# A hybrid decoder step: the selective keys of the sample tokens gathered by an on-chip list, and the differential pages loaded by SyncE

## The reference

```python
# selective (DSA): 8 heads, 2 key heads of 64; indexer with 4 heads of 64
ki_all = concat([gather_pages(cache_ik, page_table), ki])
idx, valid = select_keys(indexer_scores(qi, wi, ki_all), qpos, n_keys, 256)   # top 256 of each token
k_sel = gather_selected(cache_k, page_table, ka, idx, past)
v_sel = gather_selected(cache_v, page_table, va, idx, past)
return dsa_core(qa, k_sel, v_sel, valid, qpos[None, :, None] - idx, bias_a)

# differential: 4 heads of 2 x 64, all keys
k_all = concat([gather_pages(cache_k, page_table), kb])
v_all = concat([gather_pages(cache_v, page_table), vb])
logits = einsum('bqhcd,bkhcd->bhcqk', q, k) * 64 ** -0.5 + bias(distance)
p = softmax(where(causal, logits, -inf))
w = p[:, :, 0] - lam * p[:, :, 1]
o = rmsnorm(einsum('bhqk,bkhe->bqhe', w, v), subln_g) * (1 - lam_init)
```

## Time and profile before

| | us |
|---|---|
| median of three runs | 2603.62 |
| lowest and highest run | 2590.98, 2606.52 |
| span of the profiled execution | 2590.7 |
| PE busy | 2312.3 |
| DVE, ACT, POOL busy | 1103.6, 766.2, 660.5 |
| selective-and-sample stage, in the span | 565 to 1335 |

### The profile page before, as it was taken

How to read it: one execution, slowest core, us unless ns; L and a number is a source line. 1 busy time by engine, 2 the same in 40 slices (tenths; PEclk the granted TensorE clock), 3 DMA queues, 4 the chain that set the end, 5 groups by cost and what they waited for, 6 DMA issues and landing times. The chain is left out here.

```text
span 2590.7 us, 32530 instructions
## 1 busy us (share of the span) xinstructions
PE 2312.3 (89%) x12169; PEld 1549.6 (60%) x12189; DVE 1103.6 (43%) x2687; ACT 766.2 (30%) x2065; POOL 660.5 (25%) x703
## 2 busy tenths in 40 slices
PE   7999997767777878788789898899999999999999
PEld 5644443443455455555444445548888888888887
DVE  5489998742445533333322212352443343371001
ACT  3551345653444444444421013311111111110000
POOL 1451223123544445433301010013222121201110
PEclk9999998988889889998889999999999999999999
DMA  4211101025888778765540014111111111122221
GB/s 140 73 60 70 38 9 65 1 82 188 275 277 269 234 266 281 257 213 193 173 162 28 33 49 163 34 67 34 50 34 50 34 50 40 44 65 74 74 63 39
DMA packets 147603, 281.75 MB, mean 109 GB/s; under 512 B 13479, under 2 KB 82775, under 8 KB 147447
## 3 DMA queue, kind: packets, MB, share of 16 engines
q0 software_dynamic: 48384, 176.18, 20.2%
q1 hardware_dynamic: 80774, 90.50, 10.6%
q10 hardware_dynamic: 18288, 12.98, 1.7%
HBM read 261.68 MB, written 17.94 MB: 108 GB/s over the span
## 5 line engine op out<-in xcount | busy, mean ns | idle before, releaser
L634 PE MATMUL PS<-region 128*128 128x512 f32 (+5 forms) x864 | 327.7, 534 | 1.8 <-DMA region<-w_in 1.8
L2784 PE MATMUL PS<-region,ffn_w 128*128 128x264 f32 x1408 | 323.1, 388 | 1.6 <-PEq L2234 1.6
L2784 PEld LDWEIGHTS PS<-region,ffn_w 128*128 128x128 f32 x1408 | 269.2, 191 | 48.4 <-issue 1.9
L2004 ACT COPY region<-PS 128x512 f32<-128x512 f32 x352 | 197.2, 591 | 212.6 <-PE PS L1868 72.2
L634 PEld LDWEIGHTS PS<-region 128*128 128x128 f32 (+1 forms) x864 | 152.7, 181 | 161.2 <-issue 140.9
L2784 PE MATMUL PS<-region,side 128*128 128x264 f32 x1056 | 245.0, 389 | 1.8 <-POOL side L2741 1.8
L1875 PE MATMUL PS<-ident_f,region 128*128 128x128 f32 x1024 | 170.7, 316 | 82.4 <-ACT region L2004 44.1
L2784 PEld LDWEIGHTS PS<-region,side 128*128 128x128 f32 x1056 | 200.0, 191 | 35.8 <-POOL side L2741 1.9
L1875 PEld LDWEIGHTS PS<-ident_f,region 128*128 128x128 f32 x1024 | 133.5, 162 | 117.0 <-issue 76.3
L931 DVE TENSOR_SCALAR_CACHE_REDUCE mask<-score,cand 128x384 bf16<-128x384 f32 (+2 forms) x198 | 180.9, 942 | 3.4
L1109 POOL DMA_INDIRECT region<-cache_b_k,gather_b x128 | 120.4, 941 | 212.0 <-PE PS L1875 177.8
(11 more groups left out here) (448 smaller groups left out, 4017.7 us busy)
## 6 DMA issues: line engine op xcount, KB each, us to landing
ffn_w<-w_gate SPq DMA_DIRECT2D x11, 1024.0 KB, 5.4
ffn_w<-w_up SPq DMA_DIRECT2D x11, 1024.0 KB, 5.5
region<-w_in SPq DMA_DIRECT2D x4, 2048.0 KB, 7.9
ffn_w<-w_down ACTq DMA_DIRECT2D x7, 704.0 KB, 5.6
region<-x_prompt ACTq DMA_DIRECT2D x8, 512.0 KB, 7.1
region<-x_prompt SPq DMA_DIRECT2D x8, 512.0 KB, 10.6
mem_keys<-cache_mem_k SPq DMA_DIRECT2D x8, 512.0 KB, 5.0
mem_values<-cache_mem_v SPq DMA_DIRECT2D x8, 512.0 KB, 8.0
```

Source lines behind the costliest of these rows:

```text
L634: last = nc.tensor.matmul(M.PS[0:n, s % 3, 0:chunks[j].width], XT[:, c, t * P:t * P + n], w[j % 2][:, c, 0:chunks[j].width], start=(c == 0 ...
L2004: nc.scalar.copy(dst, M.PS[0:dst.shape[0], T0 + x % 2, 0:dst.shape[1]]).then_inc(t_read, 1)
L2784: last = nc.tensor.matmul(M.PS[:, bank, 0:TW], left[:, c, :], right[:, c, :], start=begin and c == 0, stop=(c == KH - 1), skip_group_check ...
```

## The change

Of the selective cache only three things are still read: the last page of each sequence ("near", 128 keys, with the new tokens in one chunk), and for each sample token the rows of its kept keys among the other 31 pages, 256 slots a token. A list of their row numbers is made on the chip: DVE writes the pool row number plus one of every kept key (0 elsewhere), takes out the eight largest of each of 128 partitions 32 times, counts how many each segment has, shifts the four segments' lists by the counts of the segments ahead in eight halving steps, and PE sums and turns them into columns of `ids`. These steps are "z" (41 of them); "c" and "z" steps now stand three to a chunk. POOL gathers with `ids` 128 rows of 512 B at a time: four "sets", one for each of four selective chunks (two tokens x 256 slots of four sequences), 32 gathers a set, and 16 for the near pages. The 18 selective chunks become six. Slots without a key, and the other tokens' slots, are masked by the matmul as before.

The differential pages are loaded by SP. For each page its number is loaded into a register, and a DMA brings the whole page to 128 partitions, one key of 2 KB a partition; two pages make the 256 keys of a sequence in a chunk, so a chunk takes 16 DMAs of 256 KB and 8 register loads. Keys stand now in order of pages and no longer in pairs, so the bias of the last chunk is added to the second page's columns by one matmul. The waits are those of the gathers before; the buffers stay.

The diff, cut to what the text speaks of:

```diff
-RKB, RKA, RKI = 2, 8, 16
-NCB, NCA, NCI = PAST // (P * RKB), PAST // (P * RKA), PAST // (P * RKI)
+RKB, RKI = 2, 16
+NCB, NCI = PAST // (P * RKB), PAST // (P * RKI)
...
+PAGES = PAST // PAGE
+FARW = SEGW - PAGE
@@ Setup
+        sp.dma_start(M.pages[:], io["page_table"][:]).then_inc(M.pages_loaded, 16)
...
-        if 2 <= s < 5:
-            n, rk, table = (("b", RKB, M.gather_b), ("a", RKA, M.gather_a), ("i", RKI, M.gather_i))[s - 2]
+        if s == 2:
+            link(nc.vector.tensor_scalar(M.page_rows[:], self.pt_f.rearrange("p (b i) -> p b i", i=PAGES)[:, :, PAGES - 1],
+                                         float(PAGE), K("page_row"), ALU.mult, ALU.add))
+            link(nc.vector.tensor_copy(M.gather_n[:], M.page_rows[:]))
...
+        if s == 4:
+            n, rk, table = "i", RKI, M.gather_i
@@ selective_and_sample_stage
-                       lambda step: 0.5 if step[0] in "kspof" and step[1] in selective else 1.0, lambda step: 1.0)
+                       lambda step: {"c": 0.5, "z": 0.0}.get(step[0], 2.0 if step[0] in "kspof" and step[1] in selective
+                                                             else 1.0), lambda step: 1.0)
@@ Walk
+    ROUNDS = TOPK // 8
+    LISTED = ROUNDS + 8
...
-        for kind, n_chunks in (("B", NCB), ("A", HALVES * NCA)):
+        for kind, n_chunks in (("B", NCB), ("A", 2)):
...
-        cut = iter(range(33))
+        cut = iter([("c", r) for r in range(33)] + [("z", r) for r in range(self.LISTED + 1)])
         for n in range(end + 1):
             keys = [("k", n + 1, j) for j in range(1 if self.new(n + 1) else 4)] if n < end else []
-            self.steps += keys[:3] + [("p", n)] + keys[3:] + [("o", n)] + [("c", r) for r in itertools.islice(cut, 1)]
+            self.steps += keys[:3] + [("p", n)] + list(itertools.islice(cut, 1)) + keys[3:] + [("o", n)]
+            self.steps += list(itertools.islice(cut, 1))
             if n < end:
-                self.steps += [("s", n + 1)] + [("c", r) for r in itertools.islice(cut, 1)]
+                self.steps += [("s", n + 1)] + list(itertools.islice(cut, 1))
@@ sample_attention: gpsimd
+        def near(b):
+            gather(near_k[:, b, :], near_loaded, rows_a[0], M.gather_n, b)
+            gather(near_v[:, b, :], near_loaded, rows_a[1], M.gather_n, b)
+
+        def chosen(x, v, j):
+
+            out, arrived = (set_values_at(x, j), set_values[x]) if v else (set_keys_at(x, j), set_keys[x])
+            for q in range(4):
+                t, half = 2 * (x % 2) + q // 2, q % 2
+                gather(out[:, q * P:(q + 1) * P], arrived, rows_a[v], ids,
+                       half * NS + DEC_T * (4 * (x // 2) + j) + t)
...
-        keys(0)
-        values(0)
...
+        eng.wait_ge(listed, 2)
+        for b in range(DEC_B):
+            near(b)
+        for v in range(2):
+            for j in range(4):
+                chosen(0, v, j)
+        eng.wait_ge(pv_done, walk.units[last - 2] + 1)
+        for v in range(2):
+            for j in range(4):
+                chosen(1, v, j)
+        for j in range(4):
+            eng.wait_ge(t_full, fill["k", walk.units[last], j, 1] + 1)
+            chosen(2, 0, j)
+        for j in range(4):
+            chosen(2, 1, j)
+        eng.wait_ge(pv_done, walk.units[last] + 1)
+        for v in range(2):
+            for j in range(4):
+                chosen(3, v, j)
@@ sample_attention: sync
+        def unit(u):
+
+            kind, g, c = chunks[walk.units[u]]
+            last = u == walk.n_units - 1
+            ids_b = {}
+            for v in range(2):
+                for j in range(4):
...
+                    elif v == 0:
+                        eng.wait_ge(t_full, fill["k", walk.units[u - 1], j, 1] + 1)
...
+                    elif j == 0:
+                        eng.wait_ge(pv_done, walk.units[u - 1 if last else u - 2] + 1)
+                    out, arrived = (values_at if v else keys_at)(u, j)
+                    for i in range(2):
+                        if v == 0:
+                            b = 4 * g + j
+                            ids_b[j, i] = eng.value_load(M.pages[b:b + 1, 2 * c + i:2 * c + i + 1], min_val=0,
+                                                         max_val=n_pool - 1)
+                        eng.dma_start(out[:, i * 512:(i + 1) * 512],
+                                      pages_b[v][bass.ds(ids_b[j, i], 1)].rearrange("o s f -> (o s) f")
+                                      ).then_inc(arrived, 16)
...
-                eng.wait_ge(mask_ready, 1)
+                eng.wait_ge(t_full, fill["k", walk.sets[0], 3, 0] + 1)
             else:
-                eng.wait_ge(pv_done, walk.units[-1] + 1)
+                eng.wait_ge(pv_done, walk.sets[1] + 1)
@@ sample_attention: tensor, the selective far chunks
+                for j in range(4):
+                    nc.tensor.matmul(M.PS[32 * j:32 * j + 32, L0, :], M.QBA[:, 4 * g + j, :], kt[:, j, 0:CH],
+                                     start=True, stop=True)
+                eng.wait_ge(listed, 2)
+                last = nc.tensor.matmul(out, M.tok_to_row_b[0:32, g, :], mask[0:32, c * CH:(c + 1) * CH], start=False,
+                                        stop=True, skip_group_check=True)
@@ sample_attention: vector
+        def list_kept(step):
+
+            r = step[1]
+            if r == 0:
...
+                link(nc.vector.tensor_tensor(work[:, 0:SEGW], work[:, 0:SEGW], score[:, 0:SEGW], ALU.mult))
+            elif r <= walk.ROUNDS:
+                eight = lists[0][:, 8 * (r - 1):8 * r]
+                link(nc.vector.max(eight, work[:, 0:SEGW]))
+                link(nc.vector.match_replace(work[:, 0:SEGW], eight, work[:, 0:SEGW], 0.0))
+            elif r == walk.ROUNDS + 1:
+                nc.vector.tensor_scalar(lists[1], lists[0], 0.0, 0.0, ALU.is_gt, ALU.add, accum_out=count[:, 0:1]
+                                        ).then_inc(counted_kept, 1)
...
+            if walk.ROUNDS + 3 <= r <= walk.ROUNDS + 6:
+                for k in (2 * (r - walk.ROUNDS - 3), 2 * (r - walk.ROUNDS - 3) + 1):
+                    a, b, far = lists[k % 2], lists[(k + 1) % 2], 1 << k
+                    link(nc.vector.tensor_scalar(b, a, stay[:, k:k + 1], None, ALU.mult))
+                    last = nc.vector.scalar_tensor_tensor(b[:, far:TOPK], a[:, 0:TOPK - far], bits[:, k:k + 1],
+                                                          b[:, far:TOPK], ALU.mult, ALU.add)
...
+            elif r == walk.LISTED:
...
+                nc.vector.tensor_copy(ids[:], slots_f).then_inc(listed, 1)
```

More of the change, by code:

```diff
@@ L1604, in new, with near @@
         return self.chunks[n][2] < 0
+    def near(self, n):
+        return self.new(n) and self.chunks[n][0] == "A"
     def first(self, n):
@@ L1858, in turn_keys @@
             kind, g, c = chunks[n]
+            if walk.near(n):
+                eng.wait_ge(near_loaded, 16 * 2 * DEC_B)
+                t = bank(("k", n, j, 0))
+                for q in range(4):
+                    last = nc.tensor.transpose(t[:, q * P:(q + 1) * P], near_k[:, 4 * g + q, :], K("ident"))
+                last.then_inc(t_full, 1)
+                return
             if walk.new(n):
                 return
[L1861 to L1863 removed]
             if kind == "A":
+                x = walk.sets.index(n)
+                keys = set_keys_at(x, j)
+                eng.wait_ge(set_keys[x], 16 * 16)
                 t = bank(("k", n, j, 0))
                 for q in range(4):
[L1867 to L1868 removed]
+                    last = nc.tensor.transpose(t[:, q * P:(q + 1) * P], keys[:, q * P:(q + 1) * P], K("ident"))
                 last.then_inc(t_full, 1)
                 return
+            u = walk.units.index(n)
+            keys, arrived = keys_at(u, j)
+            eng.wait_ge(arrived, 16 * walk.keys_arrivals(u))
             for x in range(2):
@@ L1882, in logits @@
             out = M.PS[:, L0, 0:w]
-            if not walk.new(n):
-                eng.wait_ge(t_read, fill["k", n, 3, 1 if kind == "B" else 0] + 1)
+            if not walk.new(n) or walk.near(n):
+                eng.wait_ge(t_read, walk.last_turned(n) + 1)
             if n:
@@ L1961, in outputs @@
             last.then_inc(pv_done, 1)
+        def list_kept(step):
+            if step not in fill:
+                return
+            if step[1] == walk.ROUNDS + 2:
+                eng.wait_ge(counted_kept, 1)
+                t = bank(step)
+                nc.tensor.matmul(t[:, 0:1], K("seg_before"), count[:, 0:1], start=True, stop=True).then_inc(t_full, 1)
+                return
+            eng.wait_ge(shifted, 1)
+            t = bank(step)
+            for half in range(2):
+                nc.tensor.matmul(t[:, half * NS:(half + 1) * NS], lists[0][:, half * P:(half + 1) * P],
+                                 K("seg_sum")[:, 0:NS], start=half == 0, stop=True, skip_group_check=half > 0)
+            nc.tensor.matmul(t[0:NS, 2 * NS:2 * NS + TOPK], K("seg_sum")[:, 0:NS], lists[0], start=False, stop=True,
```

(9 more changed lines are left out.)

295 lines of the change are left out of this document (163 added, 132 removed).

## The result

The changed kernel takes 2609.1 us (median of 8 runs), the kernel before 2597.1 us on the same chip: ratio 1.0047, 95% interval 1.0029 to 1.0066. It is slower by half a per cent (12 us); a gain of 63 us, to 2540 us, was forecast. The profiled execution took 2609.2 us, its span is 2607.4 us.

The account below looks back on a forecast made before the run. PE was taken as the limit of the differential part and mostly of the selective part. Terms -73 - 12 + 18 + 4 = -63 us, with SP loads, POOL and setup at 0, took 2603.6 to 2540 us; range 2480 to 2630.

Parts of the forecast that it names:

- The gathers do not press: Differential chunks before the change: POOL's eight gathers take 9.9 us of a 15.8 us chunk, asked for early enough.
- GpSimd: 0: POOL's near and chosen gathers at 1.24 us each: fourth set comes just in time, 0 us (bounds 0 and +20).
- Rival 3: Selective part: fourth set comes late behind POOL's 96 gathers after chunk 30, +20 us, 2560 us; 12%.
- PE works some 2.4 us a chunk longer than its rows say: Differential chunks before: late readers mean hidden PE work, 77 us over 32 chunks, so PE is the limit.
- Differential loads by SyncE, 0 us: SP's issues and register loads take 13.9 us of a 15.8 us chunk, hidden by PE: 0 us.
- rival 1: Differential chunks: SP becomes the bound if a register load takes 1.3 us, +144 us, 2684 us; 15%.
- Selective chunks -73: Selective part: fewer chunks cut PE work from 174 to 114 us, time from 213 to 140 us (bounds -105, -43).
- prompt steps -12: Differential part: 99 prompt steps instead of 105, 1.45 heads fewer, -12 us (bounds -16 and 0).
- list +18: Chunks 11 to 24: DVE's list rounds of 2.6 us sometimes delay what PE needs, +18 us (bounds 0 and 48).
- counts +4: Threshold search in the differential part: three counts a chunk instead of two, +4 us (0 to 10).
- Rival 2: List chunks: DVE becomes the bound with rounds of 4.7 us, +30 us, and heads are delayed, 2580 us; 13%.
- rival 4: Selective part: removed work was not on the path, heads' chain sets 170 us instead of 140, 2570 us; 7%.

Follow-up runs that it names:

- SP half: Kernel before with only its differential chunks loaded by SP in whole pages, selective part left on POOL: 2510.9 us, 0.970.
- before, with rests: Kernel before plus two POOL memsets of 200 columns behind each of the four value gathers of a differential chunk: 2529.5 us, 0.974.
- ten gathers: Changed kernel with 10 of its 144 gathers, most near and chosen keys and values left out, all other work kept: 2448.6 us, 0.947.
- ten gathers, no rounds: Changed kernel with 10 of 144 gathers and without the list's 32 rounds on VectorE, its rows taken from another table: 2421.5 us, 0.934.
- changed, a gather every 1.70 us: Changed kernel plus two POOL memsets of 200 columns behind each of its 144 gathers: 2503.3 us, 0.965.
- changed, every 1.54 us: Changed kernel plus two POOL memsets of 100 columns behind each gather: 2495.8 us, 0.961.
- changed, every 1.70 us, list sooner: Changed kernel, two 200-column memsets behind each gather, four search or list steps a chunk, odd chunks' last two values out of side buffers: 2474.1 us, 0.952.
- the probes: Two kernels: SP half plus unread dummy work on POOL (gathers unbroken, spaced or grouped; in one also plain DMAs and memsets): 2558 and 2596 us.

## Why the prediction was wrong

The forecast sum was -63 us; measured, the ledger reads -77 (SP half), -61 (selective part and list, without their gathers), +150 (the gathers), +12 in all (-2.98, -2.35 and +5.80% of 2594 us; each is good to some 7 to 10 us). The traces say where the time went. The differential part here runs from the first to the last logits of a differential chunk, the selective part from there to the first matmul of the output projection:

| one profiled execution each, us | differential part | selective part |
|---|---|---|
| before | 499 | 240 |
| before, with rests | 444 | 235 |
| SP half alone | 428 | 235 |
| ten gathers | 440 | 155 |
| ten gathers, no rounds | 412 | 157 |
| changed kernel | 551 | 206 |
| changed, a gather every 1.70 us | 440 | 210 |
| changed, every 1.54 us | 460 | 188 |
| changed, every 1.70 us, list sooner | 468 | 158 |

Stops lengthen the differential part by 111 us (551 against 440), and rests take all of that back. The 55 us that stay with rests lie in the selective part, where the sets come late. The changed kernel's 51 us there (206 against 155) no run takes apart.

1. **"The gathers do not press" and "GpSimd: 0"**: the steps that failed. I read POOL's row only as a supply line, by its period of 1.24 us and by when each set would be there. Its effect on others was not in the sum: 144 gathers at that period cost 150 us. Rests took 103 of them off, so the stops cost that or more; the other 48 are late sets at the slower pace that the rests bring. Rival 3 had late sets at +20 us, but at 1.24 us from gather to gather and without stops, and that case no run shows. Its sign, PE waiting for sets, is absent from the changed kernel and came only with the rests.
2. **"PE works some 2.4 us a chunk longer than its rows say"**: the same mistake, ahead of the change. The late readers in the earlier trace rows were real, and the delay had the right size, but it was no hidden work of PE: POOL's four gathers of values, back to back, stand right there (the second of them is the row at 1031.67 in the earlier trace rows; the last starts at 1034.15 and ends at 1035.1, DVE's maximum comes at 1034.66). Four rows of POOL against one gap of the three others would have shown it. Pauses took 64 us out of the kernel before; under my reading nothing could have come of them.
3. **Differential loads by SyncE, 0 us**: it was -77. SP's own time was well estimated: 12.2 us a chunk against 13.9. A register load with its address work is about (8.4 - 3.7)/8 = 0.6 us where 0.5 + 0.3 was put; rival 1 fell. The Trainium skill's floor of about 600 ns for a tensor_load (DMA: Bandwidth & Descriptors, Latency and other measured facts) is near it. What was missing was the gain from taking 256 gathers off POOL; rests alone, which leave them there, gave 64 of the 77. The same page of the Trainium skill asks for 1 MiB or more per DMA (Rules for kernel authors). Smaller ones showed no price here: 307 GB/s with 256 KB each, 261 with the 512 KB gathers, whose chunks the stops held up. The two queues' rates on which the forecast leaned were no test of it, for they mix transfers of many sizes.
4. **Selective chunks -73, prompt steps -12, list +18, counts +4**: -63 together, measured -61. Only the rounds are known by themselves: 2.43 us each, against 2.6 taken, and 27 to 32 us in the time against 18. So the other three terms together were about -90, against -81. The table agrees: 80 us less in the selective part, 12 more in the differential part, where -12 + 18 + 4 = 10 was put. Part of this is luck, for the 64 gathers of the old selective chunks, up to eight of them back to back (in the SP half's trace), went too; what their stops had cost was not in the sum, and no run shows it. Rival 2 fell by the length of a round, rival 4 by the 155 us.

That 2609 us lies inside the stated range of 2480 to 2630 is luck as well. The upper end stood for the mild end of rival 1, slow register loads, which did not happen; and of the two terms put at 0 one was -77 and the other +150, so their errors half cancelled.

## What to carry to other kernels

Look at what the other engines do while POOL issues: a gap that PE, ACT and DVE share, with "issue" or a late reader behind it, and a row of indirect gathers over it, is one thing and not four. Count instructions as well as busy time, since a lower clock makes fewer matmuls look like more work. Leave about 1.7 us from the start of one indirect gather of this kind to the next, if need be with idle work between, or move whole-page loads to SP, where a page number in a register does. Weigh this against the time until the data is needed: at 1.54 us the kernel was no slower than at 1.70, in spite of slight stops. When a busy engine is taken for the bound because its readers come late, test that by adding a pause elsewhere.

## What the runs showed of the hardware

Indirect gathers on POOL, 24 in a row at one every 1.25 us, left PE 0.00 us and ACT 0.00 us of work from the ninth us to the end. SP took up to 4.95 us for the issues of four value pages, where 1.80 is usual. The clock granted to PE stood at 0.50 in that stretch, the lower of its two levels, and was 0.88 in the 8 us ahead, in which PE ran out of work. The number of rows (32 or 128) and their width (128 or 512 bytes) made no difference to the stop; every 1.39 us it was still there, at 1.54 slight (451 matmuls for 574), at 1.70 gone, and plain DMAs of POOL every 0.54 us did nothing. The stop began some 4 to 5 us behind the first gather of a row in the probes, about 7 us behind it in the changed kernel, and 3 us behind it in the kernel before, where spaced gathers of keys stand ahead. So the four back to back in each of its chunks cost only some 2 us (64 us in 32 chunks), groups of six cost half of the matmuls (156 for 332), and groups of three little (273 for 288). The Trainium skill (GPSIMD Engine Reference, Key points) says that GpSimd shares its SBUF interfaces with VectorE; that alone would not be it, for 72 memsets of POOL left PE at 0.93, and ACT and SP stood still as well. Which resource the engines lack in a stop no run here shows. A gather's own time did not depend on its bytes: 0.94 us on POOL for 64 KB (and for 16 KB) as for 512 KB, 0.87 for 32 rows.
